# Gate scatters dealt by VectorE's work, 20 of them in the dense loop with sums 14 tiles behind, and the latent attention by pairs of heads with three buffers

## What is computed

```python
m = W_out( sig(x Wg_a) * (StickBreak(x) W_oa) + sig(x Wg_b) * (MLA(x) W_ob) )
h = LayerNorm(ALPHA * x + m)
y = LayerNorm(ALPHA * h + PEER(h))

def mla_attend(q_nope, q_pe, k_nope, k_pe, v, q_pos, k_pos):
    s = (einsum('bqhd,bkhd->bhqk', q_nope, k_nope) + einsum('bqhr,bkr->bhqk', q_pe, k_pe))
    s = s * ((MLA_NOPE_DIM + MLA_ROPE_DIM) ** -0.5)
    mask = (k_pos // CHUNK)[None, :] <= (q_pos // CHUNK)[:, None]
    p = softmax(where(mask, s, NEG_INF), axis=-1)
    return einsum('bhqk,bkhd->bqhd', p, v)

def peer(h, ...):            # 8 heads, 16 experts each, for every frame
    s1, i1 = top_k(s[:, :, 0], 16); s2, i2 = top_k(s[:, :, 1], 16)
    top_s, top_pos = top_k(all 256 sums of pairs, 16)
    g = softmax(top_s)
    act = gelu(einsum('thkd,td->thk', peer_u[experts], xb))
    return einsum('thk,thkd->td', g * act, peer_v[experts])
```

## Time and profile before

| | us |
|---|---|
| median of three runs | 3550.9 (3545.1 to 3551.6) |
| time of the profiled execution | 3558.3 |
| its span | 3556.5 |
| group 0: project, stick, mla_project, mla, merge, scores | 154.4, 29.6, 46.6, 43.8, 85.0, 77.6 |
| group 1 | 205.5, 128.0, 56.0, 120.9, 106.3, 119.0 |
| group 2 | 211.2, 190.9, 63.1, 174.0, 122.9, 106.4 |
| dense | 1515.2 |

### The profile page before, as it was taken

One profiled execution on the slowest core, in us unless ns is written; L12 is line 12 of the kernel. 1 busy time (PEld: TensorE's weight loads), 2 busy tenths in 40 slices (PEclk: granted clock), 3 DMA queues, 4 the chain that ended last, 5 costly groups with the idle time before them and its releaser, 6 DMA issues. The chain is left out here.

```text
span 3556.5 us, 36144 instructions
## 1 busy us (share of the span) xinstructions
PE 3036.3 (85%) x10170; PEld 1717.7 (48%) x10170; DVE 2536.0 (71%) x5041; ACT 1210.2 (34%) x3181; POOL 1558.1 (44%) x1184
## 2 busy tenths in 40 slices
PE   8979989676889895775887898999989999989988
PEld 5755745344545453433654554444444444444443
DVE  0122069887786877877867678888888888788886
ACT  0241234665533435754552322222222222222221
POOL 0000025667662288888777533333333333333330
PEclk9989999785789997997688999999999999999999
DMA  4675589666799997576678999999999999999995
GB/s 144 217 254 177 190 311 394 207 181 202 222 321 359 338 341 218 145 202 181 183 248 301 406 404 399 399 405 396 404 378 412 400 407 398 397 393 407 400 408 204
DMA packets 375912, 1098.51 MB, mean 309 GB/s; under 512 B 91712, under 2 KB 210208, under 8 KB 289568
## 3 DMA queue, kind: packets, MB, share of 16 engines
q0 software_dynamic: 165072, 751.05, 56.6%
q1 hardware_dynamic: 176800, 303.85, 24.4%
q10 hardware_dynamic: 33840, 41.30, 3.3%
HBM read 1031.97 MB, written 63.02 MB: 308 GB/s over the span
## 5 line engine op out<-in xcount | busy, mean ns | idle before, releaser
L428 POOL DMA_INDIRECT expert_rows<-in_experts,picked_index x640 | 770.9, 1204 | 1271.1 <-DVE ff_sum L583 1157.1
L571 DVE SCALAR_TENSOR_TENSOR expert_rows<-expert_rows,h_tile 128x1024 f32<-128x1024 f32 x672 | 820.1, 1220 | 256.8 <-DMA expert_rows<-in_experts,picked_index 212.4
L583 DVE SCALAR_TENSOR_TENSOR ff_sum<-expert_rows,coefficients,ff_sum 128x1024 f32<-128x1024 f32 x672 | 860.8, 1281 | 92.2 <-ACT coefficients L534 75.9
L1786 PE MATMUL dense_act_ps<-dense_hT,key_columns 128*128 128x384 f32 x2048 | 724.7, 510 | 139.5 <-DMA key_columns<-in_key_columns 128.5
L451 POOL DMA_INDIRECT gates_by_expert<-dense_gate,gate_address x384 | 680.3, 1772 | 154.7 <-issue 129.2
L1775 PE MATMUL dense_out_ps<-dense_value_rows,dense_weights 128*128 128x512 f32 x1536 | 678.9, 592 | 0.5 <-DVE dense_weights L1854 0.5
L1786 PEld LDWEIGHTS dense_act_ps<-dense_hT,key_columns 128*128 128x128 f32 x2048 | 399.4, 198 | 482.8 <-DMA key_columns<-in_key_columns 196.2
L833 PE MATMUL proj_ps<-xT,w_in_block 128*128 128x384 f32 (+1 forms) x1392 | 424.1, 468 | 40.7 <-PEq L1595 16.5
L1775 PEld LDWEIGHTS dense_out_ps<-dense_value_rows,dense_weights 128*128 128x128 f32 x1536 | 291.8, 190 | 342.6 <-issue 309.7
L833 PEld LDWEIGHTS proj_ps<-xT,w_in_block 128*128 128x128 f32 x1392 | 268.3, 193 | 195.7 <-issue 37.9
L528 ACT ACTIVATE activated<-dots 128x1 f32<-128x1 f32 (+1 forms) x631 | 124.8, 198 | 638.5 <-DVE expert_rows L571 601.5
(11 more groups left out here) (186 smaller groups left out, 3144.8 us busy)
## 6 DMA issues: line engine op xcount, KB each, us to landing
key_columns<-in_key_columns SPq DMA_DIRECT2D x128, 512.0 KB, 11.6
dense_value_rows<-in_experts SPq DMA_DIRECT2D x128, 512.0 KB
gates_by_expert<-zeros POOLq DMA_DIRECT2D x12, 2048.0 KB, 21.9
wq_half<-in_peer_wq SPq DMA_DIRECT2D x48, 512.0 KB
dense_gates<-gates_by_expert SPq DMA_DIRECT2D x128, 192.0 KB
w_in_block<-in_w_in ACTq DMA_DIRECT2D x18, 1024.0 KB
w_in_block<-in_w_in SPq DMA_DIRECT2D x18, 1024.0 KB
w_out<-in_w_out SPq DMA_DIRECT2D x24, 512.0 KB, 7.5
```

What stands on the lines that cost most here:

```text
L428: pool.indirect_dma_start(to, None, self.a["experts"], bass.IndirectOffsetOnAxis(ap=index[:, k:k + 1], axis=0)).then_inc(self.got[p % self ...
L571: dve.scalar_tensor_tensor(place, place, 1.0, self.h[n % 2][:], ALU.mult, ALU.mult, accum_out=self.dots[:, s % TOPK:s % TOPK + 1]).then_in ...
L583: dve.scalar_tensor_tensor(total, self.ring[:, p % self.RING, D:2 * D], self.coef[:, y % TOPK:y % TOPK + 1], total, ALU.mult, ALU.add).the ...
L1786: mm = nc.tensor.matmul(up[it % 2][:, 0:W], keys[it % KB][:, k, :], hTd[:, k, :], start=(k == 0), stop=(k == KC - 1))
```

## The change

Four things are edited.

1. **The dealing of the scatters.** The credit goes by VectorE's work: a row counts 4, a route stage 1, the sum is capped at 280, and unused credit at 1 instead of 4. The shares are new. Scatters placed in each stage before and after: group 1 project 15 and 11, stick 38 and 38, mla_project 16 and 16, mla 34 and 34, merge 25 and 24, scores 0 and 5; group 2 project 55 and 30, stick 73 and 64, mla_project 26 and 22, mla 54 and 60, merge 32 and 24, scores 16 and 36; dense 0 and 20.
2. **The dense loop** has LAG = 14, so the wait for all scatters stands at the load of tile 10 instead of 4, and there are 19 buffers of weights.
3. **The latent attention.** The factor of the scores is folded into the query gains (`gain`, one more VectorE instruction in mla_project), with a minus sign, so that the minimum of the scores is the bias as it stands. There are three score buffers of two banks, three of turned probabilities, and one bank each for turning and for the output; four key tiles are turned at a time. The product with the values takes two heads at once: 64 columns of values are the weights and 128 turned probabilities move, into the two halves of the output's partitions. So the output comes out turned, and ScalarE copies it to `obT`, undivided.
4. **The division** moves to the start of merge: the inverse sums are turned on TensorE, copied by ScalarE, spread over 64 partitions by 8 products with a broadcast column of the identity, and VectorE multiplies `obT` with them in 4 instructions, ahead of the first product that reads `obT`.

```diff
-    IDS = 192
+    IDS = 176
     SHARES = (
-        ((1, "project"), 42, 1, 9, 10), ((1, "stick"), 18, 2, 5, 38), ((1, "mla_project"), 6, 1, 1, 16), ((1, "mla"), 18, 2, 4, 34),
+        ((1, "project"), 42, 1, 9, 16), ((1, "stick"), 18, 2, 5, 38), ((1, "mla_project"), 6, 1, 1, 16), ((1, "mla"), 18, 2, 4, 34),
...
-        ((3, "dense"), 1000, 1, 24, 16),
+        ((3, "dense"), 1000, 1, 24, 60),
...
-        share = {block: gates / min(len(self.beside[block]), 90) for block, _, _, _, gates in self.SHARES}
+        work = lambda e: 4.0 * e[2] if e[0] == "rows" else 1.0
+        share = {block: gates / min(sum(work(e) for e in self.beside[block]), 280.0) for block, _, _, _, gates in self.SHARES}
         for k, (block, i, e) in enumerate(points):
-            credit += share[block]
+            credit += share[block] * work(e)
...
-            credit = min(credit, 4.0)
+            credit = min(credit, 1.0)
...
+            nc.vector.tensor_scalar(gain[:, 0:QC], gain[:, 0:QC], -MLA_SCALE, None, ALU.mult).then_inc(gain_scaled, 1)
...
+            scores(0)
+            scores(1)
+            for n in range(N + 1):
+                if n + 2 < N:
+                    scores(n + 2)
+                if n < N:
...
+                    for y, part in enumerate(parts(i)):
+                        if n or y:
+                            pe.wait_ge(t_copied, copies_before[n] + y)
+                        for x, (off, rows, vt) in enumerate(part):
+                            mm = nc.tensor.transpose(tp[0:rows, P * x:P * x + r], p[n % 2][0:r, off:off + rows], m["ident"][0:r, 0:r])
+                        mm.then_inc(t_done, 1)
+                k = n - 1
+                if k >= 0 and k % 2:
...
+                        for par in range(2):
+                            first = HD * (h - 1 + par)
+                            mm = nc.tensor.matmul(op[half[par], P * (h // 2):P * (h // 2) + r], f["mv"][0:rows, vt, first:first + HD],
+                                                  pT[(k - 1 + par) % 3][0:rows, P * x:P * x + r], start=(x == 0), stop=(x == len(tiles) - 1),
+                                                  skip_group_check=True)
...
-                    nc.vector.reduce_max(mx[0:r, t:t + 1], sp[t % 2][0:r, 0:nk], AX).then_inc(max_done, 1)
-                    dve.wait_ge(max_done, t + 1)
-                    nc.vector.tensor_scalar(nm[0:r, t:t + 1], mx[0:r, t:t + 1], -MLA_SCALE, None, ALU.mult).then_inc(nm_done, 1)
+                    nc.vector.tensor_reduce(nm[0:r, t:t + 1], sp[t % 3][0:r, 0:nk], AX, ALU.min).then_inc(nm_done, 1)
...
+            for n, t in enumerate(g.tiles):
+                mm = nc.tensor.transpose(ps[4][0:HEADS, g.at[t]:g.at[t] + r], ri[0:r, HEADS * n:HEADS * (n + 1)], m["ident"][0:r, 0:r])
...
+                    if j == 0 and i == 1:
+                        pe.wait_ge(ri_copied, 1)
+                        for q in range(4):
+                            for par in range(2):
+                                pick = m["ident"][0:HEADS, 2 * q + par:2 * q + par + 1].broadcast_to([HEADS, HD])
+                                mm = nc.tensor.matmul(ps[q][HD * par:HD * par + HD, 0:W], pick, riT[0:HEADS, :], start=True, stop=True, skip_group_check=True)
+                            mm.then_inc(spread, 1)
+                        pe.wait_ge(scaled, 4)
...
+                nc.vector.tensor_tensor(f["obT"][:, q, :], f["obT"][:, q, :], ps[q][:, 0:W], ALU.mult).then_inc(scaled, 1)
...
-        LAG, AHEAD = 8, 2
+        LAG, AHEAD = 14, 2
```

More of the change, by code:

```diff
@@ L180 @@
     SHARES = (
[L181 to L185 removed]
+        ((1, "project"), 42, 1, 9, 16), ((1, "stick"), 18, 2, 5, 38), ((1, "mla_project"), 6, 1, 1, 16), ((1, "mla"), 18, 2, 4, 34),
+        ((1, "merge"), 17, 1, 2, 24), ((1, "scores"), 27, 1, 3, 16),
+        ((2, "project"), 40, 1, 9, 44), ((2, "stick"), 26, 2, 6, 64), ((2, "mla_project"), 7, 1, 2, 22), ((2, "mla"), 25, 2, 5, 60),
+        ((2, "merge"), 20, 1, 2, 24), ((2, "scores"), 29, 1, 0, 36),
+        ((3, "dense"), 1000, 1, 24, 60),
     )
@@ L1324, in _ @@
         @block.scalar
         def _(act):
-            for t in range(N + 1):
+            for t in range(N + 2):
                 if t < N:
@@ L1353, in _ @@
-                bg.act((n + 1) / N)
+                    if n >= 3:
+                        act.wait_ge(av_done, (n - 3) // 2 + 1)
+                    for y, part in enumerate(parts(i)):
+                        act.wait_ge(t_done, copies_before[n] + y + 1)
+                        if i < TILES:
+                            nc.scalar.copy(pT[n % 3][:, 512 * y:512 * y + P * len(part)], tp[:, 0:P * len(part)]).then_inc(t_copied, 1)
+                        else:
+                            nc.scalar.copy(pT[n % 3][0:NEW, 0:r], tp[0:NEW, 0:r])
+                            for x in (1, 2):
+                                ins = nc.scalar.copy(pT[n % 3][:, P * x:P * x + r], tp[:, P * x:P * x + r])
+                                if x == 2:
+                                    ins.then_inc(t_copied, 1)
@@ L1355, in _ @@
+                n = t - 2
+                if n >= 0 and items[n][1] == HEADS - 1:
+                    i = items[n][0]
+                    r = rows_of(i)
+                    act.wait_ge(av_done, (n + 1) // 2)
+                    nc.scalar.copy(f["obT"][:, :, g.at[i]:g.at[i] + r], op[:].rearrange("p (x q) -> p x q", x=4)[:, :, 0:r]).then_inc(o_copied, 1)
+                bg.act(min(1.0, t / N))
         @block.vector
@@ L1357, in _ @@
             cut = 0
-            for t in range(N + 3):
+            for t in range(N + 2):
                 if t < N:
@@ L1559, in _ @@
         def _(dve):
+            for q in range(4):
+                dve.wait_ge(spread, q + 1)
+                nc.vector.tensor_tensor(f["obT"][:, q, :], f["obT"][:, q, :], ps[q][:, 0:W], ALU.mult).then_inc(scaled, 1)
             for j in range(KC):
```

135 lines of the change are left out of this document (45 added, 90 removed).

## The result

The changed kernel takes 3564.3 us, median of 20 runs (3554.2 to 3574.5), against 3557.5 us for the kernel before in its 20 (3541.4 to 3565.7): a ratio of 1.0025 with a 95% interval of 1.0016 to 1.0034. (The ratio isn't that of the two medians, which lie 6.8 us apart.) It is 9 us slower, where 27 us faster was forecast. Over 20 runs the kernel before has a median 7 us above that of its first three, on which the forecast of 3524 us rests, so 7 of the 40 us to that number are no error of the sum.

What follows compares the result with a forecast made beforehand. Transfers were taken to bound the dense loop, GpSimd group 2's attention. Groups 0, 1, 2 and dense: -3 - 6 - 38 + 20 = -27 us, so 3531.3, less 7.4 from profiled execution to median: 3524 us, range 3488 to 3550.

Steps and rivals of the forecast that it cites:

- The dense term: Dense loop: a stall for late scatters costs 25 us and the loop's end gains 5, together +20 us.
- The stall: Start of the dense loop: TensorE idles about 35 us after 11 ups, waiting for keys behind the last scatter's landing; 25 us lost.
- The end: End of the dense loop: 15 sums instead of 9 after the last up, with 36 us of transfers beside them; -5 us.
- Group 2's attention: Latent attention of group 2: GpSimd's list of scatters and rows decides its time; -21 us, to about 153.
- 18 brought along, less 22: Group 2's attention: GpSimd's 157.5 us of work, plus 18 of arrears brought in, less 22 carried over, gives 153.5.
- the rival in which VectorE sets the pace (E): Group 2's attention: GpSimd isn't the bound, VectorE's pace gives -39 us instead of -21; 3506 us in all, chance 0.10.
- Group 1's attention: Latent attention of group 1: VectorE loses scalings, divisions, copies and waits, and GpSimd's list fits; -18 us, to 103.
- rival C: The attentions: a chain of ScalarE and TensorE with one turning bank halves their 47 us gain; 3548 us, chance 0.15.
- Group 2's project: Project stage of group 2: 25 scatters fewer on a GpSimd that has time there; with stick -3 us at the most.
- Group 1's mla_project: Stage before group 1's attention: GpSimd's wait for a head's landing stands directly before the barrier; +8 us, to 64.
- Rival B: Dense loop: no stall, as the last scatter lands within 59 us of the loop's start; 3499 us, chance 0.20.
- Rival D: Dense loop: the wait for the scatters' landing lasts beyond T0 + 126, outweighing all gains; 3566 us, chance 0.10.

## Why the prediction was wrong

**The dense term, +20 forecast, +52 measured.** Three parts.
- The stall. Forecast: last scatter issued at T0 + 81 to 89, TensorE on at T0 + 92 to 97, 25 us lost. Measured: T0 + 93.7, T0 + 104.5, 26 us lost. This mechanism was right. Its times weren't: GpSimd came with 5 late scatters more, in arrears from scores (the trace has 25 of them in the loop, with the one under way at T0) and 21 rows for 18; a scatter took 1.88 + 0.31 us, and the line of the earlier trace rows that I took for VectorE's first row, at T0 + 12.7, is a route stage (`MAX8`). GpSimd's first wait for a place in the ring ended at T0 + 23.9. The landing took 3 us from the issue's end to SyncE's load, not 8, and TensorE idled 45.9 us, not 35. That the loss came out at 25 all the same is luck: TensorE went on 8 to 12 us later, but by then 31 MB had come, not 27.
- The second pause, 18 us, was not forecast. I had treated the background as freely available. It is due by ups and sums, and with 14 ups ahead of the first sum its supply is halved.
- The end, -5 forecast. The step that failed is "Six more [sums] carry 6 x (1.62 rows ...)": I let the rows run beside the sums to the end, when the formula for the share due, divided by 2 x 128 - 10, has them done near the last up. LAG = 14 alone measured +27 us; with the formula changed, 7. This is the largest single error. For all that LAG does beside the stall the forecast had -5; LAG alone measured +27, of which the profiles put 11 us at the end, where its sign was wrong, and 9 at the start, the kind of loss that the second pause is here.

**The foreground, -47 forecast, -48.8 measured, by luck.** The attention and division were to bring -33 and brought -7 by the timed runs, -10 in the foreground. The dealing was to bring -15 and brought -44.
- Group 2's attention: -21 forecast, -6.6 measured. GpSimd worked on without a pause; its rows in the changed kernel answer to rows 4:

```profile
L454 POOL DMA_INDIRECT gates_by_expert<-dense_gate,gate_address x65 | 111.0, 1708 | 19.8 <-issue 19.5 <-DVE ff_sum L586 0.3
L431 POOL DMA_INDIRECT expert_rows<-in_experts,picked_index x26 | 27.4, 1053 | 7.9 <-issue 7.9
```

  65 scatters and 26 rows went through, 166.1 us with the idle between them, in 167.4. The prices were right (2.01 and 1.36); the step that failed is "18 brought along, less 22": more was brought in than handed on, 5 scatters and a row. VectorE was done 12 us before the end, so the rival in which VectorE sets the pace (E) fell. That GpSimd was the bound fits the two other counts: with 70 scatters and the old attention GpSimd's list filled 186 of 188.0 us, and in the run of the attention alone, with 58 through and one pause of 11.5 us, 170 of 172.9. It isn't shown alone, since no run changes the count and nothing else, and in the changed kernel TensorE also waited 47.9 us for ScalarE's copies, VectorE only 13.7 us for rows.
- Group 1's attention: -18 forecast, -8.3 measured (-12.0 in the run of the attention alone). The waits speak for rival C's mechanism. From those of the changed kernel in group 1's attention:

```profile
PE mla_ps_turned L1307 <- ACT probsT L1346: 31.9, 19, 4.2
...
DVE score_ps L1371 <- PE score_ps L1290: 27.1, 4, 20.2
...
ACT probsT L1346 <- PE mla_ps_turned L1307: 11.3, 12, 4.6
```

  One turning bank and two halves tie TensorE to ScalarE's copy. (20.2 of VectorE's 27.1 stand at the stage's beginning, behind the barrier.) That the chain alone set this stage's end wasn't tried.
- The pair product costs 97 ns, 32.6 us for 336, not 74; still 22 us less than the 55.0 of the earlier trace rows:

```profile
L1307 PE MATMUL mla_ps_turned<-identity,probs 128*128 128x128 f32 x168 | 35.7, 341 | 47.9 <-ACT probsT L1346 47.9
L1319 PE MATMUL mla_ps_turned<-probsT,mla_v 128*64 128x128 f32 x336 | 32.6, 372 | 0.7 <-ACT probsT L1346 0.7
```

  All idle time around both forms is put down to ScalarE's copy. The Trainium skill's rule on draining at a change of tiling mode ("TensorEngine Tiling (Array Packing)", Key Properties) shows no gap of its own here; whether it is in the 23 ns more per product, no run tells.
- The division was forecast at +4 to +6 a merge and cost 6.1, 4.0 and 3.5 in the run of the attention alone.
- Group 2's project: -3 "at the most" (with stick) forecast, -21.5 measured. I took GpSimd's 134 us of work in 211 as slack. But the stage was held by the wait chain through it: VectorE waited 20 us for rows, 2.0 in the changed kernel, and TensorE was done 22.9 us before the end, 6.5 in the changed kernel. Of VectorE's waits in the kernel before, this stage:

```profile
DVE expert_rows L571 <- DMA expert_rows<-in_experts,sample_index: 15.4, 7, 3.9
...
DVE expert_rows L571 <- DMA expert_rows<-in_experts,picked_index: 4.7, 4, 1.4
```

  A share of busy time of 0.64 is no proof of slack. The rule alone gives the same 189.9.
- Group 2's mla_project: 63.1 to 51.8, as forecast (-11). Merge: -14.4 for -6; scores: +17.3 for +3.
- Group 1's mla_project: +3.7 for +8. The waiting itself was seen, but as a small change for the worse; that the stage already had some 15 us to give (41.2 by the rule alone) I hadn't seen.

Rival B (no stall) fell. Rival D's condition (the stall beyond T0 + 126) didn't come about, yet its result, 3566, nearly did, through LAG.

## What to carry to other kernels

Before a pipeline is made deeper, look what is dealt out by its position: here the background's share due, and with it the transfers that kept the queues full, hung on ups and sums, and depth emptied the queues at both ends. Where an engine may run in arrears across a barrier, keep its waits for landings away from the barrier: in two versions with the wait earlier, a stage of 56 to 60 us went to 41. And when a foreground gains by handing work to a later loop, test first what the new spacing gives without the hand-over: here the version with nothing handed over, and so with LAG back at 8, was 43 us faster than the one with 20 scatters in the loop.

## What the runs showed of the hardware

GpSimd spends 1.71 + 0.30 us on an indirect scatter of 128 single floats in group 2's attention and 1.88 + 0.31 at the start of the dense loop, but in stages shared with other work one more of them lengthened a stage by about 0.9 us. The barriers of these stages, whose blocks are made with `no_gpsimd_drain=True`, wait for GpSimd's sequencer and not for the work it has sent on: 24 us of it were seen to run on after one. A wait for a landing in front of the barrier takes that away: GpSimd's last scatter ended 5.7 us before it (824.4 and 830.1 in the changed kernel). A product of 64-column weights and 128 columns that move took 74 ns in a run of its own form and 97 ns among score and turning products.
